# First norm weight on 16 partitions and laid out by products, first weight panel in two transfers, a low part behind the norms of a delta-rule round

## What is computed

```python
def rmsnorm(x, g):
    y = xf * lax.rsqrt(jnp.mean(xf * xf, axis=-1, keepdims=True) + EPS)
    return y * g

h = jnp.concatenate([meta, x], axis=1)
u = rmsnorm(h, g_pre_mix[l])
z = u @ w_in[l]
q, k, v, xr, yr = jnp.split(z, split_at, axis=-1)
```

```python
qb = l2_norm(to_heads(q_b, N_HEADS_GDN))
kb = l2_norm(to_heads(k_b, N_HEADS_GDN))
a_low = jnp.where(strict, jnp.einsum("bhnid,bhnjd->bhnij", k_beta, k) * decay, 0.0)
sol = lax.linalg.triangular_solve(t_mat, rhs, left_side=True, lower=True, unit_diagonal=True)
attn = jnp.where(causal, jnp.einsum("bhnid,bhnjd->bhnij", q, k) * decay, 0.0)
```

## Time and profile before

| | us |
|---|---|
| median of 3 runs | 949.77 |
| lowest, highest | 949.61, 950.26 |
| the profiled execution | 954.44 |
| its span, first to last instruction | 952.7 |

### The profile page before, as it was taken

How to read it: one execution, slowest core, us unless ns; L and a number is a source line. 1 busy time by engine, 2 the same in 40 slices (tenths; PEclk the granted TensorE clock), 3 DMA queues, 4 the chain that set the end, 5 groups by cost and what they waited for, 6 DMA issues and landing times.

```text
span 952.7 us, 16712 instructions
## 1 busy us (share of the span) xinstructions
PE 903.9 (95%) x6490; PEld 844.2 (89%) x6490; DVE 604.4 (63%) x954; ACT 519.2 (55%) x903; POOL 18.5 (2%) x34
## 2 busy tenths in 40 slices
PE   4999799999997999999998989899999999999988
PEld 4988699999996999998998989899987999999966
DVE  4587855555557566767685766765668554545565
ACT  5478745454446655558355464645558544444453
POOL 1000120000000000000000000000000000000000
PEclk9999899999998999999999999999999999999989
DMA  9723686556654354554122140505574655565531
GB/s 312 244 73 101 205 170 192 176 180 190 201 178 132 124 186 143 167 177 133 46 89 90 42 135 0 174 5 177 177 232 131 223 176 180 178 209 182 180 130 44
DMA packets 106941, 144.91 MB, mean 152 GB/s; under 512 B 2968, under 2 KB 94360, under 8 KB 106896
## 3 DMA queue, kind: packets, MB, share of 16 engines
q1 hardware_dynamic: 104608, 137.60, 45.0%
q0 software_dynamic: 1968, 6.02, 2.8%
q10 hardware_dynamic: 320, 0.66, 0.2%
HBM read 143.22 MB, written 1.05 MB: 151 GB/s over the span
## 4 chain that ended last, share of the span: by engine, by line
PE 81%; DVE 10%; ACT 5%; issue 3%; DMA 1%; DVEq 0%; ACTq 0%
PE ps L1646 15%; PE ps L1648 15%; PE ps L1647 15%; PE ps L1652 8%; PE ps L1654 8%; PE ps L1653 8%; PE ps L2006 2%; PE ps L1993 2%; DVE wl L1112 2%; PE ps L2010 2%; DVE R L1390 2%; DVE R L1148 1%; ACT wh L601 1%; PE ps L1721 1%; DMA gain<-in_g_pre_mix_dram 1%
## 5 line engine op out<-in xcount | busy, mean ns | idle before, releaser
L1112 DVE TENSOR_TENSOR wl<-w_raw,wh 128x1024 fp32r<-128x1024 f32 x253 | 307.7, 1224 | 253.5 <-ACT wh L601 252.5
L1646 PE MATMUL ps<-xTh,wh 128*128 128x256 f32 (+1 forms) x1160 | 337.8, 291 | 3.9 <-DVE xTl L1138 3.9
L1647 PE MATMUL ps<-xTl,wh 128*128 128x256 f32 (+1 forms) x1160 | 329.1, 284 | 0.0
L1648 PE MATMUL ps<-xTh,wl 128*128 128x256 f32 (+1 forms) x1160 | 328.8, 283 | 0.0
L601 ACT ACTIVATE wh<-w_raw 128x1024 fp32r<-128x1024 f32 x253 | 265.2, 1052 | 89.5 <-PE ps L1654 66.2
L1646 PEld LDWEIGHTS ps<-xTh,wh 128*128 128x128 f32 x1160 | 222.5, 192 | 8.1 <-DVE xTl L1138 3.9
L1647 PEld LDWEIGHTS ps<-xTl,wh 128*128 128x128 f32 x1160 | 221.6, 191 | 1.9 <-issue 1.0
L1648 PEld LDWEIGHTS ps<-xTh,wl 128*128 128x128 f32 x1160 | 222.2, 192 | 0.0
L1652 PE MATMUL ps<-wh,y 128*128 128x512 f32 x224 | 87.7, 391 | 0.0
L1654 PE MATMUL ps<-wh,y 128*128 128x512 f32 x224 | 87.6, 391 | 0.0
L1653 PE MATMUL ps<-wl,y 128*128 128x512 f32 x224 | 87.1, 389 | 0.0
(11 more groups left out here) (349 smaller groups left out, 1275.3 us busy)
## 6 DMA issues: line engine op xcount, KB each, us to landing
w_raw<-in_w_in_dram SPq DMA_DIRECT2D x43, 1024.0 KB, 5.2
w_raw<-in_w_ff_dram SPq DMA_DIRECT2D x32, 1024.0 KB, 5.6
w_raw<-in_w_ffn_gate_dram SPq DMA_DIRECT2D x11, 1024.0 KB, 5.3
w_raw<-in_w_ffn_up_dram SPq DMA_DIRECT2D x11, 1024.0 KB, 5.3
w_raw<-in_w_ffn_down_dram SPq DMA_DIRECT2D x11, 1024.0 KB, 5.0
w_raw<-in_w_out_dram SPq DMA_DIRECT2D x8, 1024.0 KB, 4.9
w_raw<-in_w_proj_a_dram SPq DMA_DIRECT2D x4, 1024.0 KB, 5.5
w_raw<-in_w_proj_b_dram SPq DMA_DIRECT2D x4, 1024.0 KB, 5.1
```

The costliest lines, as they stand in the source:

```text
L1112: TT(low_part, raw_unit(SLOT[p], j, layout), high_part.bitcast(F32), ALU.subtract).then_inc(w_lo, 1)
L1646: mm(out, wh_, xh, start=first, stop=False)
L1647: mm(out, wh_, xl, start=False, stop=False)
L1648: return mm(out, wl_, xh, start=False, stop=last)
```

## The change

Three things change. (1) The first norm weight is loaded to 16 partitions, ahead of meta. TensorE multiplies a row of ones by it, so that PSUM (`fm`) holds it on 128 partitions; VectorE's two products of the 256 rows read it there. Meta is handled apart: GpSimd multiplies meta by the weight, VectorE takes the sum of its squares, ScalarE its root, VectorE inverts it, and ScalarE scales the product. Meta is transposed, copied and subtracted after the four pieces. (2) The first panel is loaded in two transfers, a unit each, and units 0 and 1 wait each for its own; only unit 0 is split ahead of the pieces, unit 1 behind them. (3) In a round of the delta rule the low part that belongs to c = 0 is done after VectorE's stage 1, with that of c = 1. A semaphore that nothing used goes.

```diff
+        meta_g = r_g.rearrange("p a b -> p (a b)")[0:META, 0:D]
...
-            load(P_KV, cols(w_in, 512, 1, 0))
+            kv_raw = w_raw[:, SLOT[P_KV], :].rearrange("p (k n) -> p k n", k=KC)
+            for j, landed in enumerate((k_loaded, w_loaded[SLOT[P_KV]])):
+                sp.dma_start(kv_raw[:, :, j * P:(j + 1) * P], w_in[:, 512 + j * P:640 + j * P].rearrange("(k p) n -> p k n", p=P)).then_inc(landed, 16)
...
+            pool.wait_ge(meta_loaded, 16)
+            pool.wait_ge(gain_first, 16)
+            pool.tensor_tensor(meta_g, meta[0:META, :], gain[0:META, 0, :], ALU.mult).then_inc(meta_steps, 1)
             pool.wait_ge(filled, 6)
...
-                if j == 0:
+                if pu == 0:
+                    act.wait_ge(k_loaded, 16)
+                elif j == 0 or pu == 1:
                     act.wait_ge(w_loaded[SLOT[p]], along(LOADS, p, stride // 2, i))
...
+            act.dma_start(gain[0:META, 0, :], A["g_pre_mix"][0].partition_broadcast(META)).then_inc(gain_first, 16)
             act.dma_start(meta[0:META, :], A["meta_tokens"]).then_inc(meta_loaded, 16)
             act.dma_start(ident, A["cst"][:, C_IDENT:C_TRI]).then_inc(ident_loaded, 16)
-            act.dma_start(gain[:, 0, :], A["g_pre_mix"][0].partition_broadcast(P)).then_inc(gain_first, 16)
...
                 if t == 0:
-                    act.wait_ge(meta_loaded, 16)
-                    root(meta[0:META, :], 2)
-            for n in range(2):
-                hi(n)
-            act.wait_ge(ut_ps, 1)
-            act.activation(xTh[:, :, 0:META], ma[:, 0:KC * META].rearrange("p (k n) -> p k n", k=KC), ACT.Copy).then_inc(ut_hi, 1)
+                    act.wait_ge(meta_steps, 2)
+                    act.activation(st[0:META, 6:7], st[0:META, 2:3], ACT.Sqrt, bias=eps[0:META, 0:1], scale=1.0 / D).then_inc(stat, 1)
+            act.wait_ge(meta_steps, 3)
+            act.activation(meta[0:META, :], meta_g, ACT.Copy, scale=st[0:META, 6:7]).then_inc(meta_steps, 1)
+            hi(0)
             for n in range(4):
                 piece_hi(n, META)
-            for n in range(2, 4):
+            pieces[0] += 1
+            act.wait_ge(ut_ps, pieces[0])
+            act.activation(xTh[:, :, 0:META], ma[:, 0:KC * META].rearrange("p (k n) -> p k n", k=KC), ACT.Copy).then_inc(ut_hi, 1)
+            for n in range(1, 4):
                 hi(n)
...
             dve.wait_ge(filled, 4)
-            dve.wait_ge(gain_first, 16)
+            dve.wait_ge(meta_loaded, 16)
+            link(TT(u[0:META, 1, :], meta[0:META, :], meta[0:META, :], ALU.mult))
+            dve.tensor_reduce(st[0:META, 2:3], u[0:META, 1, :], AX, ALU.add).then_inc(meta_steps, 1)
+            gain_ps = fm.rearrange("p a b -> p (a b)")
             inverse(4)
-            STT(u[:, 0, :], h[:, 0, :], st[:, 4:5], gain[:, 0, :], ALU.mult, ALU.mult).then_inc(u_ready, 1)
-            inverse(6, META)
-            STT(meta[0:META, :], meta[0:META, :], st[0:META, 6:7], gain[0:META, 0, :], ALU.mult, ALU.mult).then_inc(u_ready, 1)
+            dve.wait_ge(vec_ps, 1)
+            STT(u[:, 0, :], h[:, 0, :], st[:, 4:5], gain_ps, ALU.mult, ALU.mult).then_inc(u_ready, 1)
+            roots[0] += 1
+            dve.wait_ge(stat, roots[0])
+            dve.reciprocal(st[0:META, 6:7], st[0:META, 6:7]).then_inc(meta_steps, 1)
             inverse(5)
-            STT(u[:, 1, :], h[:, 1, :], st[:, 5:6], gain[:, 0, :], ALU.mult, ALU.mult).then_inc(u_ready, 1)
-            for n in range(2):
-                lo(n)
-            dve.wait_ge(ut_hi, 1)
+            STT(u[:, 1, :], h[:, 1, :], st[:, 5:6], gain_ps, ALU.mult, ALU.mult).then_inc(u_ready, 1)
+            lo(0)
+            for n in range(4):
+                piece_lo(n, META)
+            pieces[0] += 1
+            dve.wait_ge(ut_hi, pieces[0])
             TT(xTl[:, :, 0:META], ma[:, 0:KC * META].rearrange("p (k n) -> p k n", k=KC), xTh[:, :, 0:META].bitcast(F32),
                ALU.subtract).then_inc(ut_lo, 1)
-            for n in range(4):
-                piece_lo(n, META)
-            for n in range(2, 6):
+            for n in range(1, 6):
                 lo(n)
...
                 for s, done in enumerate(finished(weave)):
                     stage(s, a)
                     late += done
-                    if 5 <= s < 17:
+                    if 5 <= s < 17 or (weave is GDN_WEAVE and s == 0):
                         continue
...
+            pe.wait_ge(filled, 2)
+            pe.wait_ge(gain_first, 16)
+            for half in range(2):
+                last = mm(fm[:, half, :], ones[0:1, :], gain[0:1, 0, half * 512:half * 512 + 512], start=True, stop=True)
+            last.then_inc(vec_ps, 1)
             pe.wait_ge(ident_loaded, 16)
-            pe.wait_ge(u_ready, 2)
+            for n in range(4):
+                if n % 2 == 0:
+                    pe.wait_ge(u_ready, n // 2 + 1)
+                transpose_piece(u, n)
+            pe.wait_ge(meta_steps, 4)
             for k in range(KC):
                 last = pe.transpose(ma[:, k * META:(k + 1) * META], meta[0:META, k * P:(k + 1) * P], ident[0:META, 0:META])
             last.then_inc(ut_ps, 1)
-            for n in range(4):
-                if n % 2 == 0:
-                    pe.wait_ge(u_ready, n // 2 + 2)
-                transpose_piece(u, n)
+            pieces[0] += 1
```

More of the change, by code:

```diff
@@ L365, in build @@
         gain_first = sem("first_gain_loaded")
+        meta_steps, k_loaded = sem("meta_steps"), sem("first_unit_loaded")
         gain_used = sem("gain_used")
@@ L393, in build @@
                              "moba_pT0_ready", "moba_pT1_ready", "moba_o", "moba_o_hi", "moba_o_lo"))
-        cv_out, silu_qk, silu_v, sq_out, ssq_ps, rk_out, qkn_out, gb_out, gcb_ps, t12_out, dt_out, dl_out = (
+        cv_out, silu_qk, silu_v, sq_out, ssq_ps, rk_out, qkn_out, gb_out, gcb_ps, t12_out, dt_out = (
             sem(n) for n in ("gdn_conv", "gdn_silu_qk", "gdn_silu_v", "gdn_squares", "gdn_square_sums", "gdn_inv_norms", "gdn_qk_ready",
-                             "gdn_g_rows", "gdn_gc_rows", "gdn_exponents", "gdn_decay_up", "gdn_decay_low"))
+                             "gdn_g_rows", "gdn_gc_rows", "gdn_exponents", "gdn_decay_up"))
         vT_ps, kT_ps, kk_ps, kq_ps, attn_out, qeg_out, kv_out, A_out, inv_start, x0_out, xt0_ps, xt0_out = (
@@ L552, in gain_free @@
                 if n % 2 == 0:
-                    pool.wait_ge(u_ready, 3 + 4 * (n // 2 - 1))
+                    pool.wait_ge(u_ready, 4 * (n // 2) - 2)
                 else:
@@ L610, in root @@
                 act.activation(st[0:n, at + 4:at + 5], st[0:n, at:at + 1], ACT.Sqrt, bias=eps[0:n, 0:1], scale=1.0 / D).then_inc(stat, 1)
-            pieces = [1]
+            pieces = [0]
             def root_of(at):
@@ L1124, in log1p @@
                 link(TS(out, out, 2.0, None, ALU.mult))
-            roots, pieces = [0], [1]
+            roots, pieces = [0], [0]
             def inverse(at, n=P, of=st):
@@ L1166, in _ @@
             dve.wait_ge(filled, 4)
-            dve.wait_ge(gain_first, 16)
+            dve.wait_ge(meta_loaded, 16)
+            link(TT(u[0:META, 1, :], meta[0:META, :], meta[0:META, :], ALU.mult))
+            dve.tensor_reduce(st[0:META, 2:3], u[0:META, 1, :], AX, ALU.add).then_inc(meta_steps, 1)
+            gain_ps = fm.rearrange("p a b -> p (a b)")
             inverse(4)
-            STT(u[:, 0, :], h[:, 0, :], st[:, 4:5], gain[:, 0, :], ALU.mult, ALU.mult).then_inc(u_ready, 1)
-            inverse(6, META)
-            STT(meta[0:META, :], meta[0:META, :], st[0:META, 6:7], gain[0:META, 0, :], ALU.mult, ALU.mult).then_inc(u_ready, 1)
-            inverse(5)
-            STT(u[:, 1, :], h[:, 1, :], st[:, 5:6], gain[:, 0, :], ALU.mult, ALU.mult).then_inc(u_ready, 1)
-            for n in range(2):
-                lo(n)
-            dve.wait_ge(ut_hi, 1)
+            dve.wait_ge(vec_ps, 1)
[3 more added lines that the diff above has]
+            dve.reciprocal(st[0:META, 6:7], st[0:META, 6:7]).then_inc(meta_steps, 1)
+            inverse(5)
+            STT(u[:, 1, :], h[:, 1, :], st[:, 5:6], gain_ps, ALU.mult, ALU.mult).then_inc(u_ready, 1)
[4 more added lines that the diff above has]
+            dve.wait_ge(ut_hi, pieces[0])
             TT(xTl[:, :, 0:META], ma[:, 0:KC * META].rearrange("p (k n) -> p k n", k=KC), xTh[:, :, 0:META].bitcast(F32),
                ALU.subtract).then_inc(ut_lo, 1)
-            for n in range(4):
-                piece_lo(n, META)
-            for n in range(2, 6):
+            for n in range(1, 6):
                 lo(n)
-            dve.wait_ge(vec_ps, 1)
+            dve.wait_ge(vec_ps, 2)
             dve.tensor_copy(cwb, mb[:, 0:8 * LT].rearrange("p (m n) -> p m n", m=LT)).then_inc(vec_out, 1)
@@ L1853, in _ @@
             acc_tail(range(2 * P_OUT1 + 4, 2 * P_OUT1 + 8), [(yTh[:, k, :], yTl[:, k, :]) for k in range(4, 8)])
-            transposes(u, u_ready, 3)
+            transposes(u, u_ready, 2)
             F = 2 * P_FF1
@@ L1885, in _ @@
```

(4 more changed lines are left out.)

## The result

| | before | changed |
|---|---|---|
| median, us | 950.01 (4 executions) | 941.55 (4 executions) |
| lowest, highest | 949.61, 956.02 | 940.15, 942.39 |
| profiled execution, its span | 954.44, 952.7 | 941.35, 939.6 |

The ratio is 0.9895, with a 95% interval of 0.9854 to 0.9936: faster, as forecast, but 941.55 lies above the range of 928.5 to 937.5, and 8.5 us were gained where 17.9 were forecast. The two profiled executions lie 13.1 us apart. The medians lie 8.5 apart, so one of these two executions at least is far from its kernel's median; that is half of the story.

The account below looks back on a forecast made before the run. TensorE was taken as the bound, busy 95%, so only its waits and slow stretches could give time: 949.77 less 14.8 (rounds: stops 10.0, clock 4.8) and 3.1 (start) gives 931.9 us, range 928.5 to 937.5.

Parts of the forecast that it names:

- The stops at L1959: Delta-rule rounds: four TensorE waits of 11.0 us shrink by 10.6, less 0.6 of new waits for X, worth 10.0 us.
- The clock's return: Delta-rule rounds: without the long stops, three falls of TensorE's clock vanish, 1.6 us each, 4.8 us together.
- clock falls stay: Rival, chance 0.15: falls of TensorE's clock in the rounds remain despite shorter stops; time 936.7 us.
- Meta's landing: Start: meta's transfer, second at 1.19 us, lands at 4.4 us, with a bound at 6.4.
- The square: Start, VectorE: square of meta takes 1.23 us and the sum no more, together 4.45 to 6.9 us.
- The product's 2.4 us: Start, GpSimd: meta times weight takes 2.4 us, between 1.05 and 3.2, ending at 6.85 us.
- the broadcast last at 8.0 us: Start: TensorE's weight broadcast, 4.0 to 7.9 us, is the last input VectorE's first product of x awaits.
- the 3.1 us: Start: TensorE begins unit 0 at 15.35 us in place of 18.41, a gain of 3.1 us.
- The small-start rival: Rival, chance 0.12: the start gives only 1.0 us because meta or GpSimd's product is late; time 934.0 us.
- The large start: Rival, chance 0.11: the start gives 5.0 us, with broadcast at full rate and the clock up earlier; time 930.0 us.
- the cover of the loads: Start: 448 KB less brings the panel to 9.7 us and its first half to 8.3, against a need at 10.4.
- X late: Rival, chance 0.02: low parts ahead of L1418 delay X, moving TensorE's stop to L1972; 6 us late gives 955.9 us.

Follow-up runs that it names:

- The third part alone: Kernel before with only the low part of c = 0 moved behind the norms of a delta-rule round; median 939.54 us, ratio 0.9852.
- Meta first: Changed kernel with meta's transfer issued ahead of the weight's on ScalarE's queue; 938.51 us, one execution.
- meta off the path: Changed kernel with meta's root on ScalarE behind both roots of x, no square or sum on VectorE, scaling after the first piece's copy; median 934.61 us, ratio 0.9798.
- The start alone: Changed kernel with the low part of c = 0 put back ahead of the delta-rule norms; median 954.78 us, ratio 1.0022.

## Why the prediction was wrong, point by point

**The stops at L1959: right.** Forecast 10.6 us for the stops less 0.6 of new waits for X. The profile after has 0.4 us at L1981 and 1.0 us of waits of the weight loads for X in four rounds; between the two profiled executions the four rounds bring 14.4 us with the clock (from 0.6 behind to 13.8 ahead), forecast 14.8. The third part alone is 9.8 us below the quick executions of before, forecast 10.0.

**The clock's return, 4.8 us: the mechanism right, the base wrong.** This is the first step that failed. I took the term from the profiled execution (954.44 us, three falls) and subtracted it from a median of 949.77, of executions as quick as those that show no sign of these falls. The gap of 4.7 us between the two stood in front of me, "with no row that tells why", and is as large as the term of 4.8, three falls of 1.6 us. That it is nothing but these falls is not shown, since no quick execution of before has a trace; the edit that takes the stops away gained 9.8 us on the quick kind and 14.1 on the common one. Had I asked what the same sum says against the profiled execution, it would have been 936.5 to the 941.35 measured. Of these 4.8 us the start is 3.0, the rounds 0.4, and 1.4 went outside both, in small steps at the later norms (121, 313 and 921 to 930 us) and at the end. The quiet base leaves 949.8 - 10.0 = 939.8. My rival "clock falls stay" had the right size, for another reason: nothing was left there to return. That an execution may or may not have the falls was in the text, as a rule of the Trainium skill (TensorE: Matmul & The Clock Gate, What's actually happening), by which the gate's timing is not tied to the kernel's start; the 17 executions in 70 at a clock of 0.985 agree. I applied it to where falls may move to and not to the base.

**Meta's landing, 4.4 us: mis-sized.** It took 4.8 us from its issue, not 3.2. My bound of 6.4 held, in the changed kernel at least; 7.0 and 7.4 in two others did not. The row for it was the identity's 5.2 us in the second place, and I let the first place's 3.2 stand for both because meta's rows are long. Meta first showed that it is the place.

**The square, 1.2 us: mis-sized by 2.2 us.** It ran at the same time as GpSimd's product, and took 3.39 us; apart from it, 1.21. The prediction put nothing on the square for GpSimd's product beside it, though it named the Trainium skill's statement (GPSIMD Engine Reference, section 1) that the two engines contend for SBUF when VectorE has two SBUF inputs. The pair of runs agrees with the statement. The price here is 2.2 us of VectorE's time for a product of 2.3. The product's 2.4 us were right.

**What follows from these two.** The forecast had the broadcast last at 8.0 us; it was last in the kernel with meta off the path, and at 9.8 in the one with meta first. In the changed kernel the square and the sum end at 10.75 and not at 6.9, 1.6 us of it from the landing and 2.2 from the square; ScalarE's second root waits for them, and the 3.1 us are gone: 0.07 at unit 0. The small-start rival (1.0 us) had half of the cause, the late landing. The other half, a slow square, was in no rival. The large start named something else that is real, the clock up earlier in unit 0: with meta off the path it gave 1.7 us. Low part 1 behind the pieces, the broadcast's 3.75 us at the low clock (forecast 3.9), the cover of the loads and the panel's halves were as forecast.

**The rest.** 939.8 and a start worth 0 leave 1.8 us to the 941.55 measured. The start alone measures +0.2% with an interval of 0 to 0.4%, and the changed kernel is 1.4 to 2.0 us above the third part alone. Two things could do it: a later landing of meta in the timed executions (up to 1.35 us was seen), or unit 0 at the low level (1.2 us between the changed kernel's two traces). Most of the timed executions have no trace, so this part stays open. What decides when meta lands, at 6 or at 7.4, was not tried either. One sum of the rivals is off as well, without weight for the result: "X late" speaks of the clock falling again but subtracts the clock's 4.8 us. With the falls kept, slower than before needs X 3.3 us late in each round and not 4.5, and 6 us late gives 960.7 us.

## What to carry to other kernels

Before a term that comes from one profiled execution is taken off a median, ask whether that execution is of the median's kind: a gap between the two of just the size of the term may be the term, already missing from the median. When work moves to an idle engine, cost it on the engine that runs beside it too, and put the small part (16 rows here) behind the large part in every queue it shares, since whoever is late takes all behind it along. The wait that an order written by hand makes, a low part ahead of norms whose inputs were ready 2.1 us before, was worth more than the whole new start, and one line moved it.

## What the runs showed of the hardware

Two engines with two SBUF inputs each, 16 partitions by 1024 elements, at the same time: VectorE 3.38 to 3.40 us in five traces, in place of 1.21 in the two traces that keep them apart; GpSimd 2.33 to 2.34 in both cases. Two transfers of 64 KB in one queue beside large ones: 3.2 to 3.5 us for the first, 4.7 to 6.2 for the second. And the granted clock: behind stops of 2.6 to 2.9 us it fell in three cases of four in two traces and in one of four in a third, behind stops of 4.0 us in four of four, and each fall made the same stretch of TensorE's work 1.6 us longer.
